# From the second MLP to the convolution by two token halves: a schedule change at one turn of a two-model kernel

## The reference

```python
for i in range(2):
    h = rmsnorm(hres, norm_g[i, 0])
    m = diff_attention(h, ...) if i == 0 else short_conv(h, w_in[i], conv_w, w_out[i])
    hres = hres + rmsnorm(m, norm_g[i, 1])
    h = rmsnorm(hres, norm_g[i, 2])
    hres = hres + rmsnorm(square(relu(h @ w_up[i])) @ w_down[i], norm_g[i, 3])

def short_conv(h, w_in, conv_w, w_out):
    b_gate, c_gate, u = split(h @ w_in, 3)
    u = c_gate * u                       # then a causal convolution of width 3 per channel
    return (b_gate * conv(u, conv_w)) @ w_out
```

## Time and profile before

| | us |
|---|---|
| median of three runs | 1973.28 (1971.84 to 1976.45) |
| the profiled execution | 1971.16 |
| its span, first to last instruction | 1969.4 |
| TensorE busy | 1887.1 (96%) |
| VectorE busy | 1387.8 (70%) |
| ScalarE busy | 839.2 (43%) |
| GpSimd busy | 149.8 (8%) |
| mean granted clock of TensorE | 0.981 |

### The profile page before, as it was taken

How to read it: one execution, slowest core, us unless ns; L and a number is a source line. 1 busy time by engine, 2 the same in 40 slices (tenths; PEclk the granted TensorE clock), 3 DMA queues, 4 the chain that set the end, 5 groups by cost and what they waited for, 6 DMA issues and landing times.

```text
span 1969.4 us, 30367 instructions
## 1 busy us (share of the span) xinstructions
PE 1887.1 (96%) x12322; PEld 1699.5 (86%) x12322; DVE 1387.8 (70%) x2110; ACT 839.2 (43%) x1286; POOL 149.8 (8%) x126
## 2 busy tenths in 40 slices
...
GB/s 182 67 105 22 54 86 65 86 108 86 108 108 107 86 86 65 44 44 44 65 65 65 108 96 98 89 105 108 45 87 105 86 66 106 107 86 107 107 86 43
DMA packets 26085, 166.54 MB, mean 85 GB/s; under 512 B 3808, under 2 KB 4064, under 8 KB 6624
## 3 DMA queue, kind: packets, MB, share of 16 engines
...
## 4 chain that ended last, share of the span: by engine, by line
PE 46%; DVE 4%; ACT 1%; issue 0%; ACTq 0%
PE ps L2857 6%; PE ps L2858 6%; PE ps L2859 6%; PE ps L2873 4%; PE ps L2872 4%; PE ps L2871 4%; PE ps L402 4%; PE ps L404 4%; PE ps L403 4%; DVE ps L560 1%; DVE h L577 1%; DVE z_lo L511 1%; PE ps L2644 0%; PE ps L2646 0%; PE ps L2645 0%; PE ps L449 0%
## 5 line engine op out<-in xcount | busy, mean ns | idle before, releaser
L402 PE MATMUL ps<-z_hi,w_hi 128*128 128x512 f32 (+1 forms) x736 | 259.8, 353 | 31.3 <-DVE z_lo L511 28.0
L384 DVE TENSOR_TENSOR w_lo<-w_raw,w_hi 128x2048 fp32r<-128x2048 f32 x93 | 214.0, 2301 | 64.6 <-ACT w_hi L373 64.5
L403 PE MATMUL ps<-z_lo,w_hi 128*128 128x512 f32 (+1 forms) x736 | 255.3, 347 | 0.0
L404 PE MATMUL ps<-z_hi,w_lo 128*128 128x512 f32 (+1 forms) x736 | 254.8, 346 | 0.0
L2857 PE MATMUL ps<-arena,w_hi 128*128 128x256 f32 (+2 forms) x768 | 245.5, 320 | 0.5 <-DVE acc L2134 0.5
L2858 PE MATMUL ps<-arena,w_hi 128*128 128x256 f32 (+2 forms) x768 | 245.9, 320 | 0.0
L2859 PE MATMUL ps<-arena,w_lo 128*128 128x256 f32 (+2 forms) x768 | 245.4, 320 | 0.0
L373 ACT ACTIVATE w_hi<-w_raw 128x2048 fp32r<-128x2048 f32 x93 | 177.1, 1905 | 71.8 <-PE ps L404 59.0
L402 PEld LDWEIGHTS ps<-z_hi,w_hi 128*128 128x128 f32 x736 | 142.9, 194 | 56.7 <-issue 22.7
L404 PEld LDWEIGHTS ps<-z_hi,w_lo 128*128 128x128 f32 x736 | 142.5, 194 | 17.5
L403 PEld LDWEIGHTS ps<-z_lo,w_hi 128*128 128x128 f32 x736 | 143.1, 194 | 16.8 <-issue 0.7
...
## 6 DMA issues: line engine op xcount, KB each, us to landing
w_raw<-wstream SPq DMA_DIRECT2D x151, 1024.0 KB, 4.8
...
```

Source lines behind the costliest of these rows:

```text
L384: dve.tensor_tensor(w_lo[:, slot, :], w_raw[:, slot, :], w_hi[:, slot, :].bitcast(f32), ALU.subtract).then_inc(wlo, 1)
L402: pe.matmul(dst, wh, zh, start=(k == 0), stop=False)
L403: pe.matmul(dst, wh, zl, start=False, stop=False)
L404: last = pe.matmul(dst, wl, zh, start=False, stop=(k == nk - 1))
```

## The change

The last two down blocks, both norms and the first two convolution blocks run by token halves: columns 0 to 255 (half 0, the early one) and 256 to 513 (half 1). TensorE (`turn_pe`) now does eight quarters of 48 products: first down block early half, second down block early half, first late half, second late half, then B_CONV early half, B_CONV+1 early half, and both again for the late half. A down tile now fills one bank and goes round over three of a pair's four banks (`turn_tile`); the fourth keeps room for column sums and the spread root. Column sums and spreads of a half are issued inside the following quarters (`between`). VectorE, ScalarE and GpSimd have orders of their own for it (`turn_dve`, `turn_act`, `turn_sums`). The scaled product (`turn_prod`) lies in `tmp` in SBUF, where it lay in PSUM. The late half counts on semaphores that earlier stages have done with (names such as b_resid, which the rows below show by their old name, a_lo). The reciprocal of the next norm is taken by halves too.

```diff
+MANY.update({B_MLP2 + down_block(q): 4 for q in (UPS - 2, UPS - 1)})
...
+        TURN = {pi: m for m, pi in enumerate([3])}
...
+        def part_of(pi, hf):
+            return (0, 256) if hf == 0 else (256, turn_size(pi)[0])
...
+        def turn_tile(pi, f, hf, t):
+            a, e = part_of(pi, hf)
+            slot = (pair_of(turn_next(pi)) + f) % 2
+            return ps[:, 4 * slot + (turn_tiles(pi) * hf + t) % 3, 0:e - a]
...
+        def turn_square(act, pi, hf, k, pre=0):
+            a, e = in_h(pi, hf)
+            if k >= 2:
...
+            if pre:
+                act.wait_ge(*ev("resid", pi, hf, k))
+            else:
+                act.wait_ge(ps_free, tile_count(pi, hf, k))
+            src = h[:, k, a:e] if pre else ac(k)[:, a:e]
+            act.activation(sq[:, k % 2, a:e], src, ACT.Square).then_inc(ev("squared", pi, hf)[0], 1)
...
+        def turn_zhi(act, pi, hf, k):
+            zi, (a, e), (x, y) = NEXT_Z[pi], in_h(pi, hf), part_of(pi, hf)
+            act.wait_ge(*ev("resid", pi, hf, k))
+            if k == 0 and hf == 0:
+                act.wait_ge(ps_full, turn_base(pi) + 2 * turn_tiles(pi))
+            act.activation(z_hi[:, k, x:y], h[:, k, a:e], ACT.Copy, scale=smc(GAIN[zi][0], GAIN[zi][1] + k)).then_inc(ev("zhi", pi, hf)[0], 1)
...
+        def turn_act(act, pi):
+            g0, late = turn_next(pi), turn_tiles(pi) == 2
+            act_load(act, ACT.Sqrt)
+            for k in range(8):
+                turn_square(act, pi, 0, k)
+            for k in range(4 if late else 1):
+                turn_square(act, pi, 1, k)
+            turn_root(act, pi, 0)
+            if not late:
+                turn_square(act, pi, 1, 1)
+            turn_zhi(act, pi, 0, 0)
+            act_hi(act, g0 % 2, g0 // 2 + 1, turn_base(pi) + 3 * turn_tiles(pi))
+            turn_zhi(act, pi, 0, 1)
...
+            else:
+                turn_square(act, pi, 1, 2)
+                turn_square(act, pi, 1, 3)
+                turn_zhi(act, pi, 0, 2)
+                turn_square(act, pi, 1, 4)
+                turn_zhi(act, pi, 0, 3)
+                turn_square(act, pi, 1, 5)
+                turn_square(act, pi, 1, 6)
+                turn_zhi(act, pi, 0, 4)
+            turn_square(act, pi, 1, 7)
+            turn_root(act, pi, 1)
+            turn_zhi(act, pi, 0, 5)
+            turn_square(act, pi, 0, 0, 1)
+            turn_square(act, pi, 0, 1, 1)
+            turn_zhi(act, pi, 0, 6)
+            act_next(act, g0 + 1)
+            turn_square(act, pi, 0, 2, 1)
+            turn_square(act, pi, 0, 3, 1)
+            turn_zhi(act, pi, 0, 7)
+            for k in range(4, 8):
+                turn_square(act, pi, 0, k, 1)
+            for k in range(8):
+                turn_zhi(act, pi, 1, k)
+                turn_square(act, pi, 1, k, 1)
+                if k == 3:
+                    turn_pre_root(act, pi, 0)
...
+        def turn_sum(pool, pi, hf, pre):
+            a, e = in_h(pi, hf)
+            for k in range(7 + pre):
+                pool.wait_ge(*ev("squared", pi, hf, k, pre))
+                if k == 0:
+                    if hf == 0:
...
+                    pool.tensor_copy(ssum[:, a:e], sq[:, 0, a:e]).then_inc(ev("summed", pi, hf)[0], 1)
+                else:
+                    pool.wait_ge(*ev("summed", pi, hf, k - 1, pre))
+                    pool.tensor_tensor(ssum[:, a:e], ssum[:, a:e], sq[:, k % 2, a:e], ALU.add).then_inc(ev("summed", pi, hf)[0], 1)
+        def turn_sums(pool, pi):
+            turn_sum(pool, pi, 0, 0)
+            turn_sum(pool, pi, 1, 0)
+            turn_sum(pool, pi, 0, 1)
+            turn_sum(pool, pi, 1, 1)
...
+        def turn_prod(pi, hf, k):
+            a, e = part_of(pi, hf)
+            return tt(4 + k % 2, e - a)
+        def turn_scale(dve, pi, hf, k):
+            a, e = in_h(pi, hf)
+            if k == 0:
+                dve.wait_ge(*ev("spread", pi, hf))
+            if k >= 2:
+                dve.wait_ge(*ev("resid", pi, hf, k - 2))
+            elif hf:
+                dve.wait_ge(*ev("resid", pi, 0, 6 + k))
+            dve.scalar_tensor_tensor(turn_prod(pi, hf, k), ac(k)[:, a:e], smc(POST[pi][0], POST[pi][1] + k), turn_roots(pi, hf),
+                                     op0=ALU.mult, op1=ALU.mult).then_inc(ev("scaled", pi, hf)[0], 1)
...
+        def turn_add(dve, pi, hf, k):
+            a, e = in_h(pi, hf)
+            dve.wait_ge(*ev("scaled", pi, hf, k))
+            dve.tensor_tensor(h[:, k, a:e], h[:, k, a:e], turn_prod(pi, hf, k), ALU.add).then_inc(ev("resid", pi, hf)[0], 1)
...
+        def turn_zlo(dve, pi, hf, k):
+            zi, (a, e), (x, y) = NEXT_Z[pi], in_h(pi, hf), part_of(pi, hf)
+            dve.wait_ge(*ev("zhi", pi, hf, k))
+            dve.scalar_tensor_tensor(z_lo[:, k, x:y], h[:, k, a:e], smc(GAIN[zi][0], GAIN[zi][1] + k), z_hi[:, k, x:y].bitcast(f32),
+                                     op0=ALU.mult, op1=ALU.subtract).then_inc(ev("zlo", pi, hf)[0], 1)
...
+        def turn_dve(dve, pi, evict):
+            g0, late = turn_next(pi), turn_tiles(pi) == 2
+            def add(hf, k):
+                turn_add(dve, pi, hf, k)
+                if k < 7:
+                    turn_scale(dve, pi, hf, k + 1)
+            def lo(hf, k):
+                turn_zlo(dve, pi, hf, k)
+            for n in range(2 * turn_tiles(pi)):
+                evict(0, n)
+            if not late:
+                evict(1, 0)
+            turn_total(dve, pi, 0)
+            evict(1, 0 if late else 1)
+            turn_rcp(dve, pi, 0)
+            if not late:
+                evict(1, 2)
+            turn_scale(dve, pi, 0, 0)
+            add(0, 0)
+            lo(0, 0)
+            evict(1, 1 if late else 3)
+            add(0, 1)
+            dve_lo(dve, g0, g0 % 2)
+            lo(0, 1)
+            add(0, 2)
+            if not late:
+                evict(1, 4)
+                evict(1, 5)
+            lo(0, 2)
+            add(0, 3)
+            evict(1, 2 if late else 6)
+            lo(0, 3)
+            add(0, 4)
+            evict(1, 3 if late else 7)
+            lo(0, 4)
+            add(0, 5)
+            turn_total(dve, pi, 1)
+            lo(0, 5)
+            add(0, 6)
+            turn_rcp(dve, pi, 1)
+            lo(0, 6)
+            add(0, 7)
+            dve_lo(dve, g0 + 1, (g0 + 1) % 2)
+            lo(0, 7)
+            turn_scale(dve, pi, 1, 0)
+            for k in range(8):
+                add(1, k)
+                lo(1, k)
+                if k == 5:
+                    turn_pre_rcp(dve, pi, 0)
...
+        def turn_columns(pe, pi, hf):
+            a, e = in_h(pi, hf)
+            n, sums = len(turn_starts(pi, hf)), turn_sums_at(pi, hf)
+            pe.wait_ge(*ev("summed", pi, hf, 6))
+            for i, x in enumerate(turn_starts(pi, hf)):
+                pe.matmul(sums[:, i:i + 1], ssum[:, a + x:a + x + P], ones[:, 0:1], start=True, stop=True)
+            pe.wait_ge(*ev("squared", pi, hf, 7))
+            for i, x in enumerate(turn_starts(pi, hf)):
+                last = pe.matmul(sums[:, n + i:n + i + 1], sq[:, 1, a + x:a + x + P], ones[:, 0:1], start=True, stop=True)
+            last.then_inc(ev("stat", pi, hf)[0], 1)
...
+        def turn_last_block(pe, pi, f, hf, nk, z, ready, between):
+            b = turn_next(pi) - 2 + f
+            a, e = part_of(pi, hf)
+            nt, base = turn_tiles(pi), turn_base(pi)
+            for t in range(nt):
+                ready(f, hf, t)
+                before = nt * hf + t - 3
+                if before >= 0:
+                    pe.wait_ge(ps_free, base + 2 * nt * (before // nt) + nt * f + before % nt + 1)
+                dst = turn_tile(pi, f, hf, t)
+                for k in range(nk):
+                    if nk * t + k in between:
+                        between[nk * t + k]()
+                    w = (nk * t + k) * P
+                    wh, wl = w_hi[:, b % 2, w:w + P], w_lo[:, b % 2, w:w + P]
+                    zh, zl = z(0, k)[:, a:e], z(1, k)[:, a:e]
+                    pe.matmul(dst, wh, zh, start=(k == 0), stop=False)
+                    pe.matmul(dst, wh, zl, start=False, stop=False)
+                    last = pe.matmul(dst, wl, zh, start=False, stop=(k == nk - 1))
+                last.then_inc(ps_full, 1)
...
+        def turn_first_block(pe, pi, g, hf, between):
+            b, ntok = turn_next(pi) + g, turn_size(pi)[0]
+            slot = pair_of(b) % 2
+            a, e = part_of(pi, hf)
+            if hf == 0:
+                pe.wait_ge(wlo, b + 1)
+                pe.wait_ge(ps_free, turn_base(pi) + turn_tiles(pi) * (3 + g))
+            for k in range(KD):
+                if g == 0:
+                    pe.wait_ge(*ev("zlo", pi, hf, k))
+                for o in range(2):
+                    if 2 * k + o in between:
+                        between[2 * k + o]()
+                    w = (o * KD + k) * P
+                    wh, wl = w_hi[:, b % 2, w:w + P], w_lo[:, b % 2, w:w + P]
```

(41 more changed lines are left out.)

122 lines of the change are left out of this document (116 added, 6 removed).

## The result

The changed kernel takes 1976.39 us (median of 12 runs, 1972.56 to 1980.02), the kernel before 1972.88 beside it (12 runs, 1970.24 to 1976.45): ratio 1.0018, 95% interval 1.0010 to 1.0027. A second comparison, 11 runs against 33, gave 1.0020 (1.0011 to 1.0029). So it is slower, by 3.5 to 4.4 us, about as much as can be told from no change; the forecast was 1976.7.

What follows compares the result with a forecast made beforehand. VectorE's list was taken as the bound: 4.4 us gained without contention, 7.1 lost to it and 0.7 to the clock, 3.4 slower; 1974.6 for the profiled execution plus 2.1 for the median gives 1976.7 us, range 1969.0 to 1980.5.

Steps and rivals of the forecast that it cites:

- TensorE is not the bound, VectorE's list is: VectorE's steps set when B_CONV+2 opens; TensorE was to wait about 3 us before the last down tile.
- GpSimd's half add 0.72 us: Length assumed for GpSimd's half-size add of square sums; a VectorE step blocked by it costs up to 0.57 us.
- Early half 2.6 us: Contention in the early half: z_lo 1 and adds 2 to 4 1.9, sixth add 0.2, z_lo 7 0.5 us.
- First late z_hi 1.5: ScalarE's first late z_hi stands behind squares made late by GpSimd's held square sums: 1.5 us.
- Late half 3.0: GpSimd takes the port between z_lo and next add: five whole meetings and two part ones, 3.0 us.
- Gain without contention 4.4: Without contention, B_CONV+2 would open at 1429.8, 4.4 us earlier than before.
- Clock 0.7: TensorE falls to half clock around 1397.6, costing the column sums 0.7 us on VectorE's path.
- rival 3: Clock lost again in the last quarter, slowing its 48 products: 3 us more, 1979.8 us; chance 0.22.
- the three waits of VectorE's list: VectorE's waits from 1394.6: second column sums 0.7, z_hi behind the root 0.9, w_hi behind z_hi 1.1 us.
- The first (no port price): VectorE's add with the product in SBUF doesn't wait for GpSimd: 1969 to 1972 us; chance 0.18.
- The second (the add wins): VectorE's add gets the port ahead of GpSimd in the late half, saving 3 us: 1973.7; chance 0.19.
- The fourth, TensorE alone: TensorE's 51.0 us of work alone sets the end: 12.1 us gained, 1961.2 us; chance 0.02.

Runs made afterwards that it cites:

- kept busy: Changed kernel with spare products on TensorE where it waits, results never read: 1976.00 us, ratio to before 1.0020, stretch 66.09 us.
- two experiments that move one operand in opposite directions: Changed kernel with the scaled product in PSUM: ratio to before 1.0007, again 0.9994; kernel before with the product in SBUF: 1.0042.
- the best version: Changed kernel with the scaled product in PSUM and a new order of steps: 1967.08 us against 1971.76 before, ratio 0.9976.

## Why the prediction was right

By its steps, on before's time scale:

- **TensorE is not the bound, VectorE's list is.** Right: its wait before the last down tile is 3.05 us for my 3, and taking it away gained 0.6 at most.
- **GpSimd's half add 0.72 us.** Measured 0.73 to 0.75. A blocked step costs 0.53 to 0.56; I had up to 0.57.
- **Early half 2.6 us** (1.9 + 0.2 + 0.5). z_lo 1 +0.47, adds 2 to 4 +0.53 each, the sixth +0.20, z_lo 7 +0.47: 2.7.
- **First late z_hi 1.5.** 1416.78 - 1414.97 = 1.8.
- **Late half 3.0.** Five adds at +0.55 and one z_lo at +0.14: 2.9, and the part meeting of the seventh chunk was absent, since the reciprocal let GpSimd pass. Contention in all 7.4 for my 7.1; the last z_lo ends at 1432.12 - 3.13 = 1429.0 for 1428.6 and the clock's 0.7.
- **Gain without contention 4.4.** With the clock held, the stretch is 66.09 - 63.22 = 2.9 longer, so 7.4 - 2.9 = 4.5. The kernel with sums over two columns shows it without that subtraction: 63.22 - 58.82 = 4.4, with one fall of the clock and 0.4 us of the late z_hi's wait still in it.
- **Clock 0.7: too small.** I placed one fall at 1397.6. It came at 1401.8 in the first trace and 1398.1 in the second, and in both there was a second one, 58 us into the stretch, which I had as rival 3 with 0.22. It slows the last products of B_CONV, so that w_hi of B_CONV+2 starts 1.8 us behind the last z_lo instead of 1.1, and from z_lo to B_CONV+2 there are 9.2 us for my 8.3; kept busy, these are 1.1 and 8.6, so 0.3 of the difference is not the clock. Both falls together are 1.2 to 2.6.

The sum was +3.4, the stretches say +4.1 and +5.5, the runs +3.5 and +4.4. The step that was mis-sized is the clock: 0.7 in the prediction, 1.2 and 2.6 in the traces. Small slips stand beside it: the three waits of VectorE's list add up to 2.7 and not 2.6, a half add of 0.60 gives 1974.8 and not 1974.5, and the start is 0.15 late. None of them changes the account. As for luck: that the median came so near my number is owed in part to the 3 us by which executions differ anyway.

**The rivals.** The first (no port price) falls by two experiments that move one operand in opposite directions. The second (the add wins) was 0.05 us away, as stated, and didn't come. The third happened in part, for 3.4 and 6.9 us of half clock and not the whole quarter, and all falls together cost 0.5 and 1.9 us over my 0.7, not 3. The fourth, TensorE alone: even the best version has 58.36 us for its 51.0. The Trainium skill ("SBUF — State Buffer", section "Who interferes with whom") has it that VectorE contends with a GpSimd instruction that reads SBUF when it has two SBUF inputs, and not with one. The traces agree in both directions: one SBUF operand 0.42 us, two 0.96 beside GpSimd's add of 0.74 and 0.42 beside its add of 0.20.
